# Routing of a mixture of experts rebuilt: early choices, new tokens second in w_o, the matrix of slots ahead of the first transposes

## The reference

```python
x = x + g1 * (m @ w_o)
h = rmsnorm(x, norm2) * (1 + sc2) + sh2
x = x + g2 * hier_moe(h, ...)
y = rmsnorm(x, final_norm)
```

## Time and profile before

| | us |
|---|---|
| median of 3 runs | 1181.98 |
| profiled execution | 1181.74 |
| its span, first to last instruction | 1180.0 |
| PE busy | 1069.7 |
| DVE busy | 560.2 |
| ACT busy | 250.2 |
| POOL busy | 154.4 |
| mean DMA rate over the span | 192 GB/s (226.32 MB) |

### The profile page before, as it was taken

One profiled execution on the slowest core, in us unless ns is written; L12 is line 12 of the kernel. 1 busy time (PEld: TensorE's weight loads), 2 busy tenths in 40 slices (PEclk: granted clock), 3 DMA queues, 4 the chain that ended last, 5 costly groups with the idle time before them and its releaser, 6 DMA issues. The chain is left out here.

```text
span 1180.0 us, 15016 instructions
## 1 busy us (share of the span) xinstructions
PE 1069.7 (91%) x5862; PEld 703.7 (60%) x5862; DVE 560.2 (47%) x1109; ACT 250.2 (21%) x673; POOL 154.4 (13%) x299
## 2 busy tenths in 40 slices
PE   5999998999999999899999999999946998978786
PEld 3455777777777887887577777754423333322222
DVE  3123737467788494475754455443264111110126
ACT  3100010567622222464111010101110110100011
POOL 3000500012314000041100000100011211111101
PEclk8999998999999999899999999999967999998998
DMA  9995543252414443124462422359176999999975
GB/s 334 340 258 181 192 77 75 43 128 69 74 50 72 107 80 73 37 73 144 125 223 83 111 75 89 123 138 327 77 286 222 416 420 415 418 419 418 412 290 175
DMA packets 96852, 226.32 MB, mean 192 GB/s; under 512 B 21422, under 2 KB 40167, under 8 KB 84082
## 3 DMA queue, kind: packets, MB, share of 16 engines
q1 hardware_dynamic: 86998, 202.70, 52.5%
q10 hardware_dynamic: 4660, 12.75, 3.1%
q0 software_dynamic: 5120, 9.88, 2.3%
HBM read 210.60 MB, written 23.08 MB: 198 GB/s over the span
## 5 line engine op out<-in xcount | busy, mean ns | idle before, releaser
L2514 PE MATMUL ps<-w_gate_up,xT 128*64 128x512 f32 x528 | 129.5, 630 | 20.5 <-DMA w_gate_up<-w_e_up 20.5
L2514 PEld LDWEIGHTS ps<-w_gate_up,xT 128*64 128x64 f32 x528 | 41.2, 145 | 105.9 <-issue 76.8
L2676 DVE TENSOR_TENSOR act<-silu_gate,ps 128x256 f32<-128x256 f32 x17 | 7.1, 420 | 199.1 <-ACT silu_gate L2469 199.1
L695 PE MATMUL ps<-hT,w_ring 128*128 128x288 f32 x384 | 97.5, 414 | 3.7 <-PEq L105 3.7
L695 PEld LDWEIGHTS ps<-hT,w_ring 128*128 128x128 f32 x384 | 73.9, 195 | 23.9 <-issue 4.0
L2531 PE MATMUL ps<-w_down,actT 128*64 128x512 f32 x264 | 62.1, 599 | 8.8 <-DVE actT L2680 8.8
L1345 PE MATMUL ps<-hT,w_ring 128*128 128x288 f32 x264 | 67.8, 407 | 0.0
L1630 DVE SCALAR_TENSOR_TENSOR conv_y<-z_staged,convT,conv_y 128x600 f32<-128x600 f32 x72 | 59.7, 842 | 9.3 <-ACT conv_y L1080 7.5
L1345 PEld LDWEIGHTS ps<-hT,w_ring 128*128 128x128 f32 x264 | 49.4, 190 | 13.1 <-issue 0.5
L2531 PEld LDWEIGHTS ps<-w_down,actT 128*64 128x64 f32 x264 | 18.0, 136 | 41.2 <-issue 29.1
L2429 POOL DMA_INDIRECT pair_scratch<-y_block,pairs x16 | 16.0, 1003 | 200.7 <-ACT y_block L2477 200.7
(11 more groups left out here) (539 smaller groups left out, 1995.2 us busy)
## 6 DMA issues: line engine op xcount, KB each, us to landing
w_down<-w_e_down SPq DMA_DIRECT2D x32, 1024.0 KB, 23.6
w_ring<-w_in SPq DMA_DIRECT2D x15, 2048.0 KB, 13.8
w_gate_up<-w_e_gate SPq DMA_DIRECT2D x30, 1024.0 KB
w_gate_up<-w_e_up SPq DMA_DIRECT2D x30, 1024.0 KB
w_ada_slots<-w_ada SPq DMA_DIRECT2D x8, 2048.0 KB, 8.4
w_ada_slots<-w_ada SPq DMA_DIRECT2D x4, 1024.0 KB, 15.0
w_ring<-w_pa SPq DMA_DIRECT2D x2, 2048.0 KB, 7.9
w_ring<-w_pb SPq DMA_DIRECT2D x2, 2048.0 KB, 7.9
```

What stands on the lines that cost most here:

```text
L695: last = nc.tensor.matmul(psum[:, bank + hf, 0:HALF], w[:, c, 128 * q:128 * q + 128], x[:, c, HALF * hf:HALF * hf + HALF], start=c == 0, s ...
L2514: last = te.matmul(psum[side(u), s % 2, :], xT[:, s % 2, c, side(u)], gu[s % GU_BUFS][:, u, :, c, :], start=c == 0, stop=c == KC - 1)
```

## The change

- **New tokens second.** `ORDER = (0, 4, 1, 2, 3)`: w_o, norms and logits take the new tokens (tile 4) second. Routing arrays are indexed by position; `POS` maps back.
- **PE's order.** Transposes and logits of a position stand between parts of the next halves: logits after four of sixteen, or eight of sixteen records.
- **The last tile** is transposed before its norm is known: DVE scales each half of x2 with `modp[:, 2]` (`scaled`), PE transposes it, and 1/rms is applied to the logits afterwards, with the part of the logits that comes from sh2 (`constant_logits`, from a 65th row beside the new tokens) added. Its h2 for the gather is made in one DVE operation. Its square is taken in two halves.
- **Early choices.** `choose_experts`, `split_pairs` and `slot_rows_of` run for positions 0 to 2 while w_o of the last positions goes on, and for positions 3 and 4 after the last logits. Counts and tables are in two parts too (`early_counts`, `late_counts`, `table`).
- **Table without blocks.** Expert and side are found by the counts themselves (`odd` adds SIDE = 1024 for odd experts), the table for the 32 first blocks needs no division by 64. What concerns overflow blocks (`over_blocks`, `over_counts`, `over_pairs`, `over_slots`, `over_tables`, `over_table_columns`) comes after the first gather, partly in step 1.
- **The matrix of slots** (`rows_of_last`) stands ahead of the transposes of step 0 on PE.
- **Down of step 3** is loaded expert by expert: the first at once, the second after `constd`, which over_slots sets, since it lies over the routing constants.
- **POOL** no longer clears x_gathered, and clears y_last after the first two gathers.

```diff
+ORDER = (0, 4, 1, 2, 3)
+EARLY_POS = 3
+def choose_experts(nc, dve, m, r, lo, hi, part):
...
+    if part == 0:
+        step(v.tensor_reduce(gmax, glog, AX.X, ALU.max))
+        tt(gone, glog, bc(gmax, NG), ALU.is_equal)
+        first_of(gone, NG)
+        step(v.tensor_scalar(pen, gone, BIG, -BIG, ALU.mult, ALU.add))
+        tt(em.rearrange("p t (g e) -> p t g e", g=NG), elog, pen.unsqueeze(3).broadcast_to([128, n, NG, 8]), ALU.add)
+    else:
+        step(v.scalar_tensor_tensor(em, r.one[:, 0, at, :], -1e38, em, ALU.mult, ALU.add))
+    step(v.tensor_reduce(mv, em, AX.X, ALU.max))
+    tt(one, em, bc(mv, NE), ALU.is_equal)
+    first_of(one, NE)
...
+def slot_rows_of(nc, dve, m, r, lo, hi, counts):
...
+    dve.wait_ge(r.counted, 1 if lo == 0 else 2)
+    for k in range(2):
+        i = v.tensor_tensor(r.prod[:, k, at, :], r.one[:, k, at, :], counts..., ALU.mult)
...
+    for k in range(2):
+        i = v.tensor_reduce(r.v[:, k, at], r.prod[:, k, at, :], AX.X, ALU.add)
...
+    for k in range(2):
+        for p in range(lo, hi):
+            last = v.tensor_scalar(r.onehot_slot[:, k, p, :], m.slots[:, :], r.v[:, k, p:p + 1], None, ALU.is_equal)
# merge_programs, sync
+        sp.wait_ge(xwd, 2)
+        sp.wait_ge(xsq, NT + 1)
         sp.wait_ge(x2st, 16 * NT)
         load_down(sp, m, ins, 2, (4, 5))
+        sp.wait_ge(h2d, NT)
+        sp.wait_ge(h2tr, END)
+        sp.wait_ge(x4tr, 2)
         sp.wait_ge(h2st[0], 48)
         sp.wait_ge(h2st[1], 32)
         load_gate_up(sp, m, ins, 2, (4, 5))
# merge_programs, tensor
+        o_half(0, 0, whole)
+        o_half(0, 1, whole)
+        o_new(1)
+        h2_transposes(0)
+        o_half(2, 0, range(0, 2))
+        logits(0)
+        o_half(2, 0, range(2, KC))
+        for p in range(2, NT):
+            if p > 2:
+                o_half(p, 0, whole)
+            h2_transposes(p - 1)
+            if p == 3:
+                constant_logits()
+            o_half(p, 1, range(0, 4))
+            logits(p - 1)
+            o_half(p, 1, range(4, KC))
+        early_counts()
+        last_transposes(0)
+        logits(END, range(0, 4))
+        table(0, EARLY_POS)
+        last_transposes(1)
+        logits(END, range(4, KC))
+        late_counts()
+        table(EARLY_POS, NT)
# merge_programs, vector
+        second_norm(0)
+        dve.wait_ge(nld, 32 * NB)
+        v.scalar_tensor_tensor(modn[0:64, 2, :], modn[0:64, 2, :], 1.0, n2[0:64, :], ALU.add, ALU.mult).then_inc(sc2, 1)
+        dve.wait_ge(sc2, 2)
+        residual(1, 0)
+        residual(1, 1)
+        add_logits(0)
+        second_norm(1)
...
+        residual(3, 1)
+        dve.wait_ge(ld, 3)
+        choose_experts(nc, dve, m, r, 0, EARLY_POS, 0)
+        second_norm(3)
+        choose_experts(nc, dve, m, r, 0, EARLY_POS, 1)
+        residual(END, 0)
+        scaled(0)
+        split_pairs(nc, dve, m, r, 0, EARLY_POS)
+        add_logits(3)
+        slot_rows_of(nc, dve, m, r, 0, EARLY_POS, psum[:, 2, 0:96])
+        residual(END, 1)
+        scaled(1)
+        dve.wait_ge(rsd, 2 * END + 4)
+        dve.wait_ge(x4tr, 2)
+        v.scalar_tensor_tensor(h, h, rstd[:, END:], modp[:, 1, :], ALU.mult, ALU.add).then_inc(h2d, 1)
...
+        choose_experts(nc, dve, m, r, EARLY_POS, NT, 0)
+        choose_experts(nc, dve, m, r, EARLY_POS, NT, 1)
+        split_pairs(nc, dve, m, r, EARLY_POS, NT)
+        slot_rows_of(nc, dve, m, r, EARLY_POS, NT, psum[:, 3, 0:64])
...
+        v.tensor_scalar(m.pairs[:, 0:NE // 2], psum[:, 2, 128:144], -1.0, EMPTY, ALU.mult, ALU.add)
+        v.tensor_scalar(m.toks[:, 0:NE // 2], m.pairs[:, 0:NE // 2], 1, None, ALU.logical_shift_right)
# expert_programs, sync
-        sp.wait_ge(overd, 1)
-        load_down(sp, m, ins, 3, (6, 7))
+        load_down_of(sp, m, ins, 3, 0, 6)
+        sp.wait_ge(constd, 1)
+        load_down_of(sp, m, ins, 3, 1, 7)
# expert_programs, gpsimd
-        p.memset(xg[:, :, :], 0.0).then_inc(ps, 1)
-        p.memset(m.y_last[:, :], 0.0).then_inc(ps, 1)
             gather(lo)
             gather(lo + 1)
             if lo == 0:
+                p.memset(m.y_last[:, :], 0.0).then_inc(ps, 1)
# expert_programs, tensor
-            x_transposes(lo)
             if lo == 0:
                 rows_of_last()
+            x_transposes(lo)
             for s in range(lo, hi):
                 gate_up(s)
+                if s == 1:
+                    over_tables()
# expert_programs, vector
+        def over_slots():
+            step(v.tensor_scalar(q[:, :], r_[:, :], 1.0 / CAP, -(CAP - 1) / (2.0 * CAP), ALU.mult, ALU.add))
...
+            for i in range(2 * NT):
+                last = v.tensor_scalar(osl[:, i, :], m.iota[:, :], slot[:, i:i + 1], None, ALU.is_equal)
+            last.then_inc(over_hot, 1)
+            dve.wait_ge(over_hot, 1)
+            v.nop().then_inc(constd, 1)
         def run(lo, hi):
+            if lo == 0:
+                over_blocks()
+                weights()
             x_evacuate(lo)
+            if lo == 0:
+                over_counts()
+                over_pairs()
             for s in range(lo, hi):
+                if s == 1:
+                    over_slots()
                 dve.wait_ge(sgd, s + 1)
+                if s == 1:
+                    over_table_columns()
```

More of the change, by code:

```diff
@@ new lines, in keep_half @@
+        def keep_half(j):
+            act.wait_ge(x4tr, j + 1)
+            act.wait_ge(lmm, END)
+            a.copy(h2T[:, 4 * j:4 * j + 4, :].rearrange("p c t -> p (c t)"), psum[:, 4 + j, :]).then_inc(h2ev, 1)
+        square(0)
+        for p in range(1, END):
+            store_h2(p - 1)
+            keep_h2T(p - 1)
+            square(p)
+        store_h2(END - 1)
+        keep_h2T(END - 1)
+        square_half(0)
+        keep_half(0)
+        square_half(1)
+        keep_half(1)
+        store_h2(END)
@@ L2175, in tensor, with o_half @@
-        o_tile(0)
-        for t in range(1, NT):
-            o_tile(t)
-            h2_transposes(t - 1)
-            logits(t - 1)
-        h2_transposes(NT - 1)
-        logits(NT - 1)
+        def o_half(p, j, cs):
+            tile, i = ORDER[p], 2 * p + j
+            if i >= 4 and cs[0] == 0:
+                pe.wait_ge(oev, i - 3)
+            for c in cs:
+                last = te.matmul(psum[:, i % 4, :], mT[:, c, tile_cols(tile)], wo[j][:, c, :], start=c == 0, stop=c == KC - 1)
+            if cs[-1] == KC - 1:
+                last.then_inc(omm, 1)
@@ new lines, in late_counts, with table @@
+        def late_counts():
+            pe.wait_ge(r.chosen, 2)
+            te.matmul(psum[:, 3, 0:32], r.strict, both[:, 3, :], start=False, stop=False)
+            te.matmul(cut(psum[:, 3, 32:96]), r.onesb, two(both[:, 3, :]), start=False, stop=False)
+            te.matmul(psum[:, 3, 32:64], r.strict, both[:, 4, :], start=False, stop=False)
+            te.matmul(psum[:, 3, 64:96], r.onesb, both[:, 4, :], start=False, stop=True).then_inc(r.counted, 1)
+        def table(lo, hi):
+            pe.wait_ge(r.hot, 1 if lo == 0 else 2)
+            for p in range(lo, hi):
+                rows = PROWS[p]
+                for k in range(2):
+                    for x in range(2):
+                        last = te.matmul(psum[:, 2, 128:144], r.onehot_slot[0:rows, k, p, :], r.parts[0:rows, x, k, p, :],
+                                         start=p == k == x == 0, stop=p == END and k == x == 1)
+            if hi == NT:
+                last.then_inc(r.tabled, 1)
@@ new lines, in tensor @@
+        whole = range(KC)
+        o_half(0, 0, whole)
[14 more added lines that the diff above has]
+            o_half(p, 1, range(4, KC))
```

560 lines of the change are left out of this document (327 added, 233 removed).

## The result

The changed kernel takes 1189.8 us (median of 7 runs, 1184.36 to 1191.07); the kernel before, beside it, 1182.22 (7 runs, 1178.93 to 1184.88). The ratio is 1.0054, 95% interval 1.0036 to 1.0071: slower by 6.4 us (4.3 to 8.4). The predicted sign is right and the size is not: +2.65 was forecast, and the median lies above the stated range, which ended at 1188.5. The profiled executions differ by less, 1185.88 against 1181.74, +4.1.

A forecast was written before the change was run, and what follows sets the result against it. The prediction took the step-3 weight stream's start to bound the kernel: gate_up(0) ending at 900.4 + 8.3 wait + 2.5 extra bytes = 911.2 against 908.56, +2.65 us, so 1184.4 us; range 1177.5 to 1188.5.

The forecast's parts named there:

- What bounds the kernel: A weight stream beginning when step-3 weights are issued, full until 1117, with the tail behind it; its start sets the end.
- Part 1: w_o with new tokens second: mod_new landed at 810.0, PE stands 2.8 us, last w_o sum at 863.7.
- Part 2: From the last w_o sum to the first gather: +16.3 us, toks at 880.0, where it was 29.8 us.
- Part 3: The first gather, beside weight transfers: 9.4 us within bounds 4.6 and 11.3, landed at 889.7.
- Part 4: rows_of_last ahead of step-0 transposes, hidden by the gather, ending 889.0; then gate_up(0) in 7.4 us.
- G: End of step 0's gate and up matmuls, freeing the step-3 weight buffer; forecast 900.4, 8.1 us earlier than 908.5.
- Part 5: SP's queue after gate_up(0): waiting for `constd` delays step-3 weights 8.3 us; second w_down half adds 2.5 to the stream.
- the forecast case: End of gate_up(0) from 897.5 to 903, giving 1181.5 to 1187 us; chance 0.60.
- rival C: PE's clock down through transposes and gate_up(0) (9.46), gather 11.3 us: total 1188.4; chance 0.13.
- A: Not slower: fast first gather, mod_new no obstacle, clock stays up; stream starts 3.5 us earlier, 1178.3; chance 0.15.
- B: The `constd` wait doesn't hold the stream, since buffers set the end; 8.1 us kept, 1173.6; chance 0.07.
- D: Gather lands before rows_of_last ends by sharing engines evenly; 889.0 sets the step, 0.7 us earlier: 1183.7; chance 0.05.

The follow-up runs named there:

- before_start_late: Kernel before, with step-3 w_gate_up issued only after DVE's product of step 1; +7.3 us by medians, ratio 1.0073.
- four_edits: Changed kernel with half_late, new_first, rows_second and gather_alone together; lowest median measured, 0.94% below the kernel before.
- half_late: Changed kernel with the wait for `constd` and the second w_down half of step 3 put behind step-3 w_gate_up; median 6.0 us below the changed kernel's.
- gather_alone: Changed kernel with gate and up of step 2 and first w_down half of step 3 issued only after the first gather landed; ratio 1.0066 to before.
- slots_early: Changed kernel with over_slots, which sets `constd`, moved from step 1 to before the loop over steps; ratio 0.9993 to before, unaltered 1.0037.
- after_again: The changed kernel measured again, unaltered; median 1185.78 us, ratio 1.0037 to the kernel before; its profiled execution took 1187.81.
- warm: Changed kernel with 24 filler transposes on PE ahead of rows_of_last; ratio interval 1.0008 to 1.0045, not told from the changed kernel's.
- rows_second: Changed kernel with rows_of_last back behind the transposes of the first gathered rows; ratio 1.0033 to before, changed kernel 1.0037.
- new_first: Changed kernel with mod_new's loads landed before the experts' first weights are issued; 2.9 us faster than changed by medians, 3.3 by ratios.

## Why the prediction came out as it did

- **What bounds the kernel** was right, and it is what the whole forecast stands on. Nine further executions of the changed kernel and its variants, with starts from 892 to 912, have streams of 210.8 to 211.3 us. The others differ by bytes: a megabyte less (before, 208.6), bytes moved while the stream was held (before_start_late, 205.7), and, as far as the trace tells, bytes still to be moved when it began (four_edits, 213.2). In time, the runs show the same direction with 5 to 6 us for the 8.9 of half_late and 7.3 to 8.6 for the 10.2 of before_start_late.
- **Part 1** was right in kind and 0.4 us off at its end (864.1 for 863.7), by errors that cancelled: mod_new could be used at 811.4 instead of 810.0, PE stood 3.96 instead of 2.8, and the rest of w_o took 43.9 us for 44.9, 1.4 of them counted for the clock. The 1.4 was read from one stop of 1.1 us near 834; the same stop near 814 left the next half tile (at 817.02) at 7.11 us, a row the prediction doesn't use.
- **Part 2** gave toks at 880.0 and it came at 880.01, which is luck as to the last tenths: from the last w_o sum it is 15.9 us for 16.3, and that made up for Part 1's 0.4.
- **Part 3** was right: 9.5 us for 9.4. The Trainium skill's rule of turns ("DMA: Bandwidth & Descriptors", Queues, rings and completion order), as I had worked it out, by which it would have been 7.1, did not show. That working took one row for one packet, where the page speaks of packets of several descriptors each, so the 9.5 refutes the working and does not test the rule. gather_alone adds what I hadn't seen: with rows_of_last ending at 890.6 the gather's length didn't decide.
- **Part 4 is the step that failed.** I took rows_of_last at 3.6 us, the slot rows at 2.65 and gate_up(0) at 7.4, because "PE has worked from 885.4 with short stops". They took 4.37 and 4.82, 3.24, and 8.78 and 9.49. PE had stood 6.44 us for the slot rows at half clock, and the stop of 1.41 for the evacuation of xT, which rows_of_last used to cover, kept the clock down or brought it down again. I had even the row for it, the half tile of 8.81 us behind a stop of 1.1, used it in Part 1, and did not apply it here, where the change itself had created the stop. And the 3.6 of the earlier trace rows was the length of rows_of_last behind the transposes, ending as the clock rose (0.50 until 900 in that trace, 0.91 in 900:901); put first, it ran at half clock. G came at 901.8 and 903.8 instead of 900.4. In the first trace the transposes began 0.8 late and took 1.16 for 2.0, the stop was 1.41 for 1.3 and gate_up(0) took 1.4 more than counted, +1.4 together; in the second the start was 1.2 late, the transposes took the 2.0 and gate_up(0) 2.1 more, +3.4. The slot rows (3.24) ran beside POOL's memset of y_last, for which I had counted a loss of 0 out of bounds up to 0.98; 0.6 was right.
- **Part 5** was right: 8.6 us for 8.3, and 2.4 for 2.5. half_late and slots_early show that it is this wait which holds the stream.
- **The sum** with measured sizes: 901.8 + 8.6 + 2.4 = 912.8 against 908.56, +4.2, and the two profiles differ by 4.1. With the second trace's G it is +6.2, and that execution took 6.1 more. Against the +2.65 forecast, Part 4 thus accounts for nearly all that the two profiled executions show; of the measured values, +4.4 (2.5 to 6.3) holds both and +6.4 (4.3 to 8.4) the second. So the forecast case and rival C, its condition half met (the clock down, the gather not at 11.3), were two ends of one thing that differs from execution to execution, and I had placed the value near the wrong end.
- **The rivals.** A failed at its first two conditions (gather 9.5, mod_new late). B is refuted by half_late. D's order occurred without its reason: rows_of_last ended after the gather had landed (890.57 and 889.97) and set the step, not because the gather was faster but because rows_of_last was later.
- **Where the routing's 11 us went:** toks came 11.0 earlier; rows_of_last behind its late input, the stop after the transposes and the half clock in gate_up(0) took 4.3 of them back by G (G - toks is 21.8 where it was 17.5; the slower gather lay in the shadow of rows_of_last), the wait for `constd` 8.6, the second half of w_down in the stream 2.4. 11.0 - 4.3 - 8.6 - 2.4 = -4.3.
- **Open:** why four of the first seven runs lie at 1189.8 or more. No profile exists of such an execution. after_again's second trace explains 1187.8 by the clock in step 0; that the rest is more of the same, or a late start of w_o, is only argued.

## What to carry to other kernels

Where the DMA engines are full from one issue to the end, a kernel's time is the time of that issue plus its bytes; look in the issuing engine's queue for what is ahead of that issue, and put every wait that guards something less urgent behind it. When a step is taken off an engine's path, ask what it had covered: here 20 matmuls had kept PE busy while xT was evacuated, and without them the stop and the half clock cost about as much as they had. And of several repairs, test them together as well as singly: the faster gather was worth nothing alone, and in the version with the lowest median it set the step.

## What the runs showed of the hardware

- PE's granted clock was at half (0.50, which is 1.2 GHz) from 880 to 889 in the changed kernel, in which PE stood 6.44 us, rose to 1.00 while it did rows_of_last and the transposes, and was at 0.50 again in 894:895 behind the stop of 1.41. In warm it was 1.00 in 888:892, with 24 filler transposes ahead, and 0.79 in 892:896, behind stops of 0.68 and 1.41 us. Without the stop gate_up(0) took 7.09 us (before, rows_second, four_edits); in the nine traces with the 1.41 us stop ahead of it, 8.71 to 9.49. A stop of 1.10 us did less surely the same: in the kernel before it stands three times ahead of logits with w_o records behind them, and the clock fell after one of the three only (the next half tile took 8.81 us, and 7.11 after another).
- A gather of 128 rows took 4.6 us in idle DMA engines (before) and 9.5 beside a weight stream at 417 GB/s (the changed kernel).
- Ten slot-row operations on DVE took 3.24 us beside a memset on POOL (one of the ten took 1.13, the others 0.33), where they took 2.65 without it (before).
- The small loads of mod_new were usable at 811.4 when the weights of step 0 were issued beside them, 27.5 us after w_o's start, and at 808.5 or earlier, 21.7 after it, when those weights waited (new_first).
